# Adaptive modulation moved from TensorE, in the mixers, to GpSimd, in the feed-forwards

## The chip, the cores and the metric

One core of one Trainium2 chip. The metric is the device time of the whole program in microseconds; lower is better. The engines are TensorE (PE; its weight load is listed apart as PEld), VectorE (DVE), ScalarE (ACT), GpSimd (POOL) and SyncE (SP), each with its own instruction stream; they are ordered against each other by semaphores alone, all written out by hand.

## The reference

Two blocks of depth 2 run one after the other on 256 rows of 1024 numbers, all in float32. The first has, per layer, a feed-forward, a hybrid mixer (forgetting attention, stick-breaking attention, a sparse attention with an index step) and a second feed-forward. The second block has neighbourhood attention with a pooling branch in layer 0 and a short convolution in layer 1, each between two feed-forwards, and these are modulated by two condition vectors:

```python
def adaln(cond, w, b):
    m = jax.nn.silu(cond) @ w + b          # cond (D,), w (D, 9*D)
    return m.reshape(m.shape[:-1] + (N_MOD, D_MODEL))

def ffn_sublayer(h, m, g, w13, w2, base):
    hn = modulate(rms_norm(h, g), m[:, :, base], m[:, :, base + 1])
    return h + 0.5 * m[:, :, base + 2] * swiglu_2(hn, w13, w2)

for i in range(DEPTH):
    m_l = adaln(c[:, None, :], mod_w[i], mod_b[i])      # mod_w (2, 1024, 9216)
    m_c = adaln(c_ctx[None, None, :], mod_w[i], mod_b[i])
```

So the modulation is a product of two vectors (`c` and `c_ctx`) with a 1024 x 9216 matrix per layer: 75.5 MB of weights for few arithmetic operations. Of `c_ctx` only the first five of nine parts of layer 0 are needed. Nothing of the modulation depends on the first block, so it may be computed at any time before the second.

## The kernel before

Everything stays in SBUF but the weights. These stream through a ring of three buffers, `raw`, of 1 MB each (a "unit"), loaded from SyncE's queue. Each unit is split into a high and a low part: ScalarE copies it to `whi` (line 415) and VectorE subtracts (`wlo = raw - whi`, line 428, two inputs in SBUF). TensorE then makes each product as three (`three`, line 710: hi by hi, hi by lo, lo by hi). Plain f32 products show in the trace as two passes.

A feed-forward (nine in all) is a loop over 11 groups of 256 hidden columns. One step is three units: two for gate and up, one for down, 72 products of 512 columns. Units of a step are split while earlier ones are used.

The phases of the program stand in a list; every engine walks it. A `norm`, `ffn` or `final` may begin before the phase ahead is over; others wait for all. In a mixer, TensorE's steps of attention are short and wait for other engines, so pieces of other work are put between them by hand: `Beside` holds a list of pieces and `PACE` says how many go at each point. There are three kinds, in the order of the string `BESIDE`:
- `D`, a part of the remaining input projection: 6 products of 512 columns, 4 such per unit, 80 per layer;
- `m`, a modulation vector of 256 columns for both conditions: 8 products with the `silu` of the conditions (`CT`, 32 columns, in four column groups of TensorE at once) as the stationary side and the weights (`mraw`, which lies in the idle tile `C`) as the moving one, then a copy by VectorE (line 1438). The weights come as two loads of 0.5 MB from SyncE's queue (line 605);
- `t`, the turn of that vector so that it lies along the partitions: two products on TensorE (line 772), a sum and the bias on VectorE (lines 1444 and 1445) into `modc`. The next `m` in a mixer waits until that has been read (`settle(unread, "row_read")`).

26 `m` and 26 `t` lie in each of the two hybrid mixers, 20 and 20 in the neighbourhood attention, where no projection is left over. In a hybrid mixer 5 pairs fall before the softmax heads, 12 beside these and 9 beside the stick-breaking heads; the 80 `D` fall 34, 24 and 22. `gains` in a feed-forward (line 1527) multiplies the norm's gains in. GpSimd has the lower 896 columns of a mixer's splits (line 671) and a few small loads.

## Time and profile before

| | |
|---|---|
| median of 3 runs | 2875.26 us (2868.48 to 2882.46) |
| the profiled execution | 2875.02 us |
| its span, first to last instruction | 2873.2 us, mean granted clock 0.958 |
| TensorE busy | 2660.1 us (93%) |
| VectorE, ScalarE, GpSimd busy | 1416.9, 1175.5, 111.3 us |
| products of the modulation, busy | 96.4 us, and 31.6 us of turns |

The nine feed-forwards take about 170 to 190 us each, some 1560 us. The hybrid mixers' attention parts run from 236 to 494 and from 960 to 1217, the neighbourhood attention from about 1984 to 2122. A time is read against the span; the time of an execution is 1.8 us more. "Busy" counts overlapping instructions of an engine once; the mean of one instruction can be longer than its share, since TensorE's are pipelined.

### The profile page before, as it was taken

The numbers are of one execution on the slowest core, as the hardware profiler recorded it, in microseconds if no ns is written. First come the engines' busy times: TensorE is split into PE (matmuls) and PEld (weight loads), VectorE is DVE, ScalarE is ACT, GpSimd is POOL, SyncE is SP. The second block draws the span as 40 slices with busy tenths as digits, with TensorE's granted clock in tenths as the row PEclk, the third lists the DMA queues.
The fourth block names the chain that finished last, engine by engine and source line by source line (L and its number), as shares of the span: only waits on it lengthen the run. The fifth ranks groups of instructions, "written<-read, shape, count | busy, mean of one in ns | idle before, by whom it ended". The sixth has DMA issues, their size and how long they took to land.

```text
span 2873.2 us, 34247 instructions
## 1 busy us (share of the span) xinstructions
PE 2660.1 (93%) x12829; PEld 2107.3 (73%) x12829; DVE 1416.9 (49%) x1830; ACT 1175.5 (41%) x1356; POOL 111.3 (4%) x85
## 2 busy tenths in 40 slices
PE   7999987899999898889989989988889999998998
PEld 6877655688788665568878878875467878876786
DVE  4555334655545643365454454443335555455554
ACT  4445334444443533444444344443024444444433
POOL 0002110000000211000000001000000000000000
PEclk9999999999999999899999999997889999998999
DMA  6556554465555555546545559842555545554453
GB/s 202 189 172 201 174 191 163 147 201 189 165 185 177 185 191 192 167 153 214 187 134 183 185 135 193 213 145 95 169 165 163 188 156 191 185 166 135 162 187 113
DMA packets 367783, 496.16 MB, mean 173 GB/s; under 512 B 14478, under 2 KB 295338, under 8 KB 367562
## 3 DMA queue, kind: packets, MB, share of 16 engines
q1 hardware_dynamic: 365338, 487.99, 51.8%
q0 software_dynamic: 2064, 5.84, 2.3%
q8 instruction: 64, 1.05, 0.2%
q10 hardware_dynamic: 288, 1.05, 0.1%
q14 instruction: 29, 0.24, 0.0%
HBM read 493.77 MB, written 1.05 MB: 172 GB/s over the span
## 4 chain that ended last, share of the span: by engine, by line
PE 85%; DVE 7%; ACT 4%; DMA 3%; issue 1%; ACTq 0%; DVEq 0%; SPq 0%; PEldq 0%
PE ps L710 79%; PE ps L790 2%; DVE wlo L428 2%; PE ps L909 2%; DMA C<-in_mod_w_dram 1%; ACT whi L415 1%; PE ps L797 1%; PE ps L772 1%; DMA raw<-in_w_in_dram 1%; ACT L1319 0%; DVE arena L1473 0%; DMA raw<-in_even_w_out_dram 0%; ACT work L1160 0%; DVE HTlo L1363 0%; DVEq L348 0%
## 5 line engine op out<-in xcount | busy, mean ns | idle before, releaser
L428 DVE TENSOR_TENSOR wlo<-raw,whi 128x2048 fp32r<-128x2048 f32 (+5 forms) x405 | 872.0, 2155 | 611.6 <-ACT whi L415 609.4
L710 PE MATMUL ps<-whi,HThi 128*128 128x512 f32 (+2 forms) x2360 | 956.2, 405 | 33.6 <-DVE HTlo L1479 16.8
L415 ACT ACTIVATE whi<-raw 128x2048 fp32r<-128x2048 f32 (+4 forms) x405 | 752.7, 1860 | 467.9 <-PE ps L710 437.8
L710 PE MATMUL ps<-wlo,HThi 128*128 128x512 f32 (+2 forms) x2360 | 929.6, 394 | 0.0
L710 PE MATMUL ps<-whi,HTlo 128*128 128x512 f32 (+2 forms) x2360 | 929.5, 394 | 0.0
L710 PEld LDWEIGHTS ps<-whi,HThi 128*128 128x128 f32 x2360 | 452.0, 192 | 155.9 <-issue 45.8
L710 PEld LDWEIGHTS ps<-wlo,HThi 128*128 128x128 f32 x2360 | 450.9, 191 | 96.4
L710 PEld LDWEIGHTS ps<-whi,HTlo 128*128 128x128 f32 x2360 | 452.6, 192 | 84.6
L710 PE MATMUL ps<-whi,AThi 128*128 128x512 f32 x792 | 310.1, 391 | 1.1
L710 PE MATMUL ps<-wlo,AThi 128*128 128x512 f32 x792 | 308.6, 390 | 0.0
L710 PE MATMUL ps<-whi,ATlo 128*128 128x512 f32 x792 | 308.1, 389 | 0.0
L710 PEld LDWEIGHTS ps<-whi,AThi 128*128 128x128 f32 x792 | 148.7, 188 | 34.8 <-issue 4.7
L1229 ACT ACTIVATE AThi<-ps 128x512 fp32r<-128x512 f32 x99 | 59.1, 597 | 278.4 <-PE ps L909 278.4
L710 PEld LDWEIGHTS ps<-wlo,AThi 128*128 128x128 f32 x792 | 148.7, 188 | 31.1
L710 PEld LDWEIGHTS ps<-whi,ATlo 128*128 128x128 f32 x792 | 148.8, 188 | 30.2
L1541 DVE TENSOR_TENSOR ATlo<-ps,AThi 128x512 fp32r<-128x512 f32 x99 | 68.3, 690 | 143.7 <-ACT AThi L1229 143.7
L710 PE MATMUL ps<-C,CT 128*32 128x256 f32 x1152 | 96.4, 454 | 42.4 <-DVE modc L1445 26.6
L1136 ACT ACTIVATE work<-ps,small 128x128 f32<-128x128 f32 (+2 forms) x60 | 29.5, 492 | 217.2 <-DVE small L1395 217.0
L1225 ACT ACTIVATE arena<-ps 128x256 f32<-128x256 f32 x110 | 36.2, 381 | 185.9 <-PE ps L710 185.9
L671 POOL TENSOR_TENSOR wlo<-raw,whi 128x896 fp32r<-128x896 f32 x36 | 84.0, 2333 | 391.7 <-ACT whi L415 391.7
L1225 ACT ACTIVATE arena<-ps,small 128x256 f32<-128x256 f32 x88 | 36.9, 470 | 140.8 <-PE ps L710 140.7
L1394 DVE TENSOR_REDUCE small<-ps 128x1 f32<-128x128 f32 (+2 forms) x60 | 26.8, 446 | 132.0 <-PE ps L790 87.8
(191 smaller groups left out, 1589.0 us busy)
## 6 DMA issues: line engine op xcount, KB each, us to landing
raw<-in_ffn_w_dram SPq DMA_DIRECT2D x330, 512.0 KB, 4.5
raw<-in_w_ffn_gu_dram SPq DMA_DIRECT2D x176, 512.0 KB, 4.7
C<-in_mod_w_dram SPq DMA_DIRECT2D x144, 512.0 KB, 4.5
raw<-in_w_ffn_down_dram SPq DMA_DIRECT2D x88, 512.0 KB, 4.0
raw<-in_w_in_dram SPq DMA_DIRECT2D x40, 1024.0 KB, 7.3
raw<-in_even_w_in_dram SPq DMA_DIRECT2D x12, 1024.0 KB, 5.1
raw<-in_conv_w_in_dram SPq DMA_DIRECT2D x12, 1024.0 KB, 5.1
raw<-in_w_out_dram SPq DMA_DIRECT2D x8, 1024.0 KB, 5.0
```

Source lines behind the costliest of these rows:

```text
L415: i = nc.scalar.activation(whi[0:rows, r, a:b], raw[0:rows, r, a:b], ACT.Copy)
L428: i = nc.vector.tensor_tensor(wlo[0:rows, r, a:b], raw[0:rows, r, a:b], whi[0:rows, r, a:b].bitcast(F32), ALU.subtract)
L671: nc.gpsimd.tensor_tensor(wlo[at], raw[at], whi[at].bitcast(F32), ALU.subtract).then_inc(s_lo_pool, 1)
L710: return nc.tensor.matmul(o, lhsT, rhs, start=first, stop=last)
L772: i = nc.tensor.transpose(ps[:, turned, k * P:(k + 1) * P], mrow[:, k * P:(k + 1) * P], ident)
L790: i = nc.tensor.matmul(S[:, o:o + ow], lh, rh, start=False, stop=j == len(mine) - 1)
L797: i = nc.tensor.transpose(T[:, c * P:(c + 1) * P], prob[(n - 1) % 2][:, c * P:(c + 1) * P], ident)
L909: i = nc.tensor.transpose(ps[:, 2, c * SEQ + b * P:c * SEQ + (b + 1) * P], av[:, b, c * P:(c + 1) * P], ident)
L1136: A(prob[n % 2][:, 0:it["n"]], ps[:, n % 2, 0:it["n"]], ACT.Exp, bias=nmx[:, n:n + 1], scale=SCALE, accum_out=rsum[:, n:n + 1]).then_inc(s ...
L1225: A(sg[:, b, :], ps[:, b, 0:GW], ACT.Silu, scale=scale).then_inc(sem("ffn_silu"), 1)
L1229: A(AT[own][0][:], ps[:, 2, :].rearrange("p (c t) -> p c t", c=2), ACT.Copy).then_inc(sem("ffn_act_hi"), 1)
L1541: V.tensor_tensor(AT[own][1][:], ps[:, 2, :].rearrange("p (c t) -> p c t", c=2), AT[own][0][:].bitcast(F32), ALU.subtract).then_inc(sem("f ...
```

## The change

All 72 vectors leave TensorE's streams in the mixers, and `BESIDE`, `m` and `t` are gone; `PACE` now counts `D` alone. GpSimd makes the vectors during the first eight feed-forwards: 10, 6, 8, 12 (layer 0), then 10, 10, 8, 8 (layer 1). It loads half of a vector's weights (4 x 128 rows by 256 columns) from its own queue, multiplies each of the four blocks by the condition's column (`tensor_scalar`), adds the blocks, and adds both halves into `acc`: 128 x 256 partial sums, one row per partition. For the first 20 vectors of layer 0 it does so for both conditions, so there are 92 such sums. Vector i of a feed-forward begins no earlier than a step given by the count of used units. TensorE waits at the end of each such feed-forward until its vectors are made. The sum over the partitions is then made by TensorE: 128 columns of `acc` as the stationary side, a column of ones as the moving one, 184 products of one column in six places. VectorE adds the bias and multiplies the gains in (`mod_add`). The bias tiles of the neighbourhood attention are now loaded between the vectors of the sixth feed-forward.

```diff
-BESIDE = ("mDDDDDDDDt" * 4 + "mDtDmDtDmDtDmDtD" * 5 + "mDtDmDDDtDDD",) * 2 + ("m" + "tm" * 19 + "t",)
-PACE = (dict(prepare=8, latent=(4, 2), turn_index=3, index=(4, 4, 4, 4, 4, 3), softmax=4, item=(2,), stick=6),) * 2 + (dict(item=(2, 2, 3)),)
+PACE = dict(prepare=7, latent=(3, 2), turn_index=2, index=(3, 3, 3, 3, 3, 3), softmax=3, item=(1,), stick=3)
...
+        mods = [modulation(l, first, last, slots[f]) for f, (l, first, last) in enumerate(
+            ((0, 0, 10), (0, 10, 16), (0, 16, 24), (0, 24, 36), (1, 0, 10), (1, 10, 20), (1, 20, 28), (1, 28, 36)))]
+        made_by = [sum(len(acc) for part in mods[:f + 1] for _, _, acc in part) for f in range(len(mods))]
+        shares = {f: (made_by[f], [x for g in fs for x in mods[g]])
+                  for f, fs in ((0, (0,)), (2, (1, 2)), (3, (3,)), (4, (4,)), (5, (5,)), (7, (6, 7)))}
...
-                        elif what == "mod":
-                            load_mod(m)
-                            load_mod(m + 1)
...
+            def modulate(ph, at, beside):
+
+                part = ph["mods"]
+                for i in range(2):
+                    mod_load(part, i, at)
+                for i in range(2 * len(part)):
+                    _, m, accs = part[i // 2]
+                    if i % 2 == 0:
+                        pool.wait_ge(s_used, ph["u0"] + 3 * (10 * (i // 2) // len(part)) + 2)
+                        beside(i // 2)
+                    halves[0] += 1
+                    pool.wait_ge(s_mod[i % 2], 16 * ((halves[0] + 1) // 2))
+                    for st, acc in reversed(list(enumerate(accs))):
+                        w = mod_raw[at][i % 2]
+                        o = w if st == 0 else mod_product
+                        for c in range(4):
+                            k = 4 * (i % 2) + c
+                            p = nc.gpsimd.tensor_scalar(o[:, MOD * c:MOD * (c + 1)], w[:, MOD * c:MOD * (c + 1)],
+                                                        cond[:, k, st:st + 1], None, ALU.mult)
+                        link(p)
+                        link(nc.gpsimd.tensor_tensor(o[:, 0:2 * MOD], o[:, 0:2 * MOD], o[:, 2 * MOD:4 * MOD], ALU.add))
+                        if i % 2 == 0:
+                            link(nc.gpsimd.tensor_tensor(acc, o[:, 0:MOD], o[:, MOD:2 * MOD], ALU.add))
+                        else:
+                            link(nc.gpsimd.tensor_tensor(acc, acc, o[:, 0:MOD], ALU.add))
+                            link(nc.gpsimd.tensor_tensor(acc, acc, o[:, MOD:2 * MOD], ALU.add))
+                    if i % 2:
+                        pool.sem_inc(s_made, len(accs))
+                    if i + 2 < 2 * len(part):
+                        mod_load(part, i + 2, at)
...
+            def mod_sums(share, bank):
+
+                settle(summed, "mods_added")
+                made, parts = share
+                pe.wait_ge(s_made, made)
+                at = 0
+                for _, m, accs in parts:
+                    for k in range(MOD // P):
+                        for acc in accs:
+                            i = mm(ps[:, bank, at:at + 1], acc[:, k * P:(k + 1) * P], cc("ones"))
+                            at += 1
+                i.then_inc(sem("mods_summed"), 1)
...
                 if ph["gate"]:
                     take("gate_read")
+                if ph["mods"]:
+                    pe.wait_ge(s_made, made_by[f])
+                if ph["sums"]:
+                    mod_sums(ph["sums"], 3)
...
                     turn(rest_chunks(), "rest_turned", ("rest_read", "rest_read"))
+                    mod_sums(ph["sums"], 5)
                     take("forget_log")
...
                     beside.go(next(quota))
+                    mod_add(ph["sums"], 5)
                     take("forget_summed")
```

GpSimd's stream at the first feed-forward, where it had nothing; after the change (`arena` holds the weights, the products and the partial sums):

```order
L660 DMA arena<-in_mod_w_dram 128x4x256
L679 TENSOR_SCALAR arena<-arena,cond 128x256 x4
L682 TENSOR_TENSOR arena<-arena 128x512
L684 TENSOR_TENSOR arena<-arena 128x256
L679 TENSOR_SCALAR arena<-arena,cond 128x256 x4
L682 TENSOR_TENSOR arena<-arena 128x512
L684 TENSOR_TENSOR arena<-arena 128x256
```

That is the first half of one vector for both conditions; the second half has one more addition of 256 for each. The first feed-forward has ten such vectors.

TensorE in the neighbourhood attention, before: the four score products of an item, `m` (`C,CT`), `t` (L772), the turns of the item ahead (L797) and its value products (128x64):

```order
L710 MATMUL ps<-arena 128x256
L790 MATMUL ps<-arena,cst 128x256
L790 MATMUL ps<-cst 128x256
L710 MATMUL ps<-arena 128x256
L797 MATMUL ps<-cst,work 128x128 x4
L710 MATMUL ps<-arena,work 128x64 x4
L710 MATMUL ps<-C,CT 32x256 x8
L772 MATMUL ps<-cst,work 128x128 x2
L710 MATMUL ps<-C,CT 32x256 x8
```

And after:

```order
L742 MATMUL ps<-arena 128x256
L816 MATMUL ps<-arena,cst 128x256
L816 MATMUL ps<-cst 128x256
L742 MATMUL ps<-arena 128x256
L823 MATMUL ps<-cst,work 128x128 x4
L742 MATMUL ps<-arena,work 128x64 x4
L742 MATMUL ps<-arena 128x256
```

Nothing stands between the items any more.

TensorE at the end of a hybrid mixer's index step, layer 0, before: the turns of the heads (L727), the forget gate's sums (128x6), its turn (L1037), then `m`:

```order
L772 MATMUL ps<-cst,work 128x128 x2
L727 MATMUL ps<-cst,arena 128x128 x16
L727 MATMUL ps<-cst,arena 64x128 x2
L727 MATMUL ps<-cst,arena 128x128 x4
L727 MATMUL ps<-cst,arena 64x128 x2
L710 MATMUL ps<-small,cst 128x6 x3
L1037 MATMUL ps<-cst,small 6x128 x2
L710 MATMUL ps<-C,CT 32x256 x8
```

And after:

```order
L759 MATMUL ps<-cst,arena 128x128 x16
L759 MATMUL ps<-cst,arena 64x128 x2
L759 MATMUL ps<-cst,arena 128x128 x4
L759 MATMUL ps<-cst,arena 64x128 x2
L742 MATMUL ps<-cst,arena 128x1 x40
L742 MATMUL ps<-small,cst 128x6 x3
L1070 MATMUL ps<-cst,small 6x128 x2
```

40 one-column products now stand ahead of the gate's sums; 48 do in layer 1.

## Rows read from the trace of the kernel before

**Rows 1.** Stretches: length, busy us (x instructions) per engine, granted clock, DMA share, GB/s.

```profile
core 0: us, PE busy (x) PEld busy (x) DVE busy (x) ACT busy (x) POOL busy (x), PEclk, DMA share, GB/s
24.00:213.00 189.00, 185.38 (x832) 152.30 (x832) 95.12 (x74) 80.07 (x72) 0.00 (x0) 0.99 0.55 182
...
312.00:412.00 100.00, 96.51 (x607) 63.92 (x611) 39.98 (x124) 30.07 (x61) 12.57 (x6) 0.98 0.64 211
412.00:494.00 82.00, 62.27 (x368) 42.92 (x365) 29.75 (x75) 34.88 (x47) 6.33 (x3) 0.86 0.49 159
...
1460.00:1498.00 38.00, 27.26 (x115) 22.19 (x114) 19.39 (x28) 20.35 (x32) 0.00 (x0) 0.82 0.22 73
...
2005.00:2126.00 121.00, 101.23 (x626) 60.35 (x626) 38.19 (x105) 12.21 (x32) 0.00 (x0) 0.77 0.54 174
```

**Rows 2.** Chain of waits, second feed-forward: start, us, what.

```profile
604.44 16.35 PE ps L710 x72
621.22 16.35 PE ps L710 x72
```

**Rows 3.** Timeline of one feed-forward step: start, us, engine, line, instruction.

```profile
606.91 2.29 DVE L428 TENSOR_TENSOR wlo<-raw,whi 128x2048 fp32r<-128x2048 f32 x1 [1.11 <-ACT whi L415]
...
614.96 0.19 PEld L710 LDWEIGHTS ps<-whi,AThi 128*128 128x128 f32 x1
```

**Rows 4.** Instruction groups: busy us, mean ns, idle before and releaser.

```profile
L710 PE MATMUL ps<-C,CT 128*32 128x256 f32 x1152 | 96.4, 454 | 42.4 <-DVE modc L1445 26.6 <-DMA C<-in_mod_w_dram 11.2 <-DVEq L348 2.1
...
L702 POOL DMA_DIRECT2D work<-in_pool_w_dram x1 | 0.8, 754 | 0.0
...
L1818 POOL MEMSET const-float32-1.0<- 128x1 f32 x1 | 0.1, 98 | 0.0
```

**Rows 5.** Timeline, softmax heads.

```profile
320.61 1.07 PE L710 MATMUL ps<-C,CT 128*32 128x256 f32 x16
...
321.61 0.50 PE L710 MATMUL ps<-whi,HThi 128*128 128x512 f32 x1
...
325.42 0.39 PE L772 MATMUL ps<-cst,work 128*128 128x128 f32 x2
```

**Rows 6.** Waits of TensorE from 412 to 494: us, times, longest.

```profile
PE ps L710 <- DVE modc L1445: 9.6, 2, 5.7
```

**Rows 7.** Timeline, stick-breaking heads, of ScalarE and of TensorE.

```profile
432.07 0.49 ACT L1317 ACTIVATE work<-ps 128x384 f32<-128x384 f32 x1
...
437.79 0.52 ACT L1326 ACTIVATE work<-work 128x384 f32<-128x384 f32 x1 [1.46 <-DVE work L1738]
...
445.80 0.49 ACT L1317 ACTIVATE work<-ps 128x384 f32<-128x384 f32 x1 [5.68 <-PE ps L710]
...
430.80 0.92 PE L710 MATMUL ps<-arena 64*128 64x256 f32 x4
...
433.36 1.07 PE L710 MATMUL ps<-C,CT 128*32 128x256 f32 x16
```

**Rows 8.** Timeline, neighbourhood attention, items at either speed.

```profile
2001.02 1.22 PE L710 MATMUL ps<-arena 64*128 64x256 f32 x2
...
2007.97 1.94 PE L710 MATMUL ps<-C,CT 128*32 128x256 f32 x16
...
2042.74 0.70 PE L710 MATMUL ps<-arena 64*128 64x256 f32 x2
...
2046.48 1.07 PE L710 MATMUL ps<-C,CT 128*32 128x256 f32 x16
```

**Rows 9.** Timeline, TensorE at the end of layer 0's index step.

```profile
304.14 0.80 PE L710 MATMUL ps<-small,cst 128*128 128x6 f32 x6 [1.45 <-ACT arena L1117]
```

**Rows 10.** Timeline, splits of VectorE and GpSimd side by side.

```profile
249.36 4.53 DVE L428 TENSOR_TENSOR wlo<-raw,whi 128x1152 fp32r<-128x1152 f32 x2
...
292.71 2.02 DVE L428 TENSOR_TENSOR wlo<-raw,whi 128x1152 fp32r<-128x1152 f32 x1
...
249.55 3.13 POOL L671 TENSOR_TENSOR wlo<-raw,whi 128x896 fp32r<-128x896 f32 x1 [3.47 <-ACT whi L415]
...
291.38 2.13 POOL L671 TENSOR_TENSOR wlo<-raw,whi 128x896 fp32r<-128x896 f32 x1 [25.11 <-ACT whi L415]
```

More of the change, by code:

```diff
@@ L252, in program @@
                       for n0 in range(0, 3 * D, 512)]
-            phase("beside", first=len(units), pieces=pieces(BESIDE[l], w, later), pace=PACE[l], end=len(units), banks=(5, 5),
-                  after=0 if l == 0 else c_read)
+            phase("beside", first=len(units), pieces=pieces(w, later), end=len(units))
             for kind in ("prepare", "latent", "turn_index", "index", "softmax", "stick"):
-                phase(kind, l=l)
+                phase(kind, l=l, sums=shares[2 * l] if kind == "index" else None)
             phase("beside_end")
@@ L303, in program @@
                 phase("near_turn")
-                phase("beside", first=len(units), pieces=pieces(BESIDE[2]), pace=PACE[2], end=len(units), banks=(6, 7), after=c_read)
                 phase("near")
-                phase("beside_end")
                 phase("turn", src=[[work[:, 2048 + b * 512 + k * P:2048 + b * 512 + (k + 1) * P] for b in range(NB)]
@@ L1026, in _ @@
                         i.then_inc(sem("index_dots"), 1)
-                    beside.go(sum(beside.pace["index"]))
+                    beside.go(sum(PACE["index"]))
                     settle(taken, "group_taken")
```

255 lines of the change are left out of this document (126 added, 129 removed).

## The prediction

> **What bounds the kernel now.** I read the stretches first. In a feed-forward TensorE is the bound: the chain of waits goes through 72 matmuls per step, one step in 16.78 us (604.44 to 621.22), with VectorE and ScalarE beside it [rows 2]. No modulation work stands there. It stands elsewhere: in a mixer's first part (236 to 312), its softmax heads (312 to 412) and its stick-breaking heads (412 to 494), all three again in layer 1, and the neighbourhood attention (2005 to 2126). TensorE is busy for 96.5 of 100 us in the softmax heads, 62 of 82 in the stick-breaking heads, 101 of 121 in the neighbourhood attention, at a granted clock of 0.77 [rows 1]. So the time of the modulation can be bought only there. The price is paid in the feed-forwards, where GpSimd now does nothing (24 to 213, POOL 0.00 [rows 1]), and where TensorE now waits at the end until GpSimd is through.
>
> **What is removed.** 72 vectors of 256 columns, each 16 products (8 f32 matmuls of two passes; 1152 in all, 16 a vector), one copy and, later, two turns and two small VectorE operations [rows 4]. In TensorE's stream a piece m takes 1.00 us (320.61 to 321.61) and its turn t about 0.25 us of its 0.39, the rest being overlap [rows 5]: 1.25 us for a pair. A mixer holds 26 of them: 5 in the first part, 12 in the softmax heads, 9 in the stick-breaking heads.
> - Softmax heads: TensorE-bound, so 12 x 1.25 = 15 us per layer. What is late next is an item's exponential. It comes from VectorE's maximum of the item before, 0.29 to 0.42 us, and ScalarE's 0.47 us, while TensorE has a projection piece of 1.4 us and its own 2 us to do: covered.
> - First part: 5 x 1.25 = 6 us, and about 3 us in which TensorE waits for the turned row to be read: 9 us per layer.
> - Stick-breaking heads: one head now takes 13.7 us (ScalarE's first step at 432.07, then at 445.80) [rows 7]. In these heads TensorE waits for a modulation row to be read by VectorE, which is behind its head's own chain: 9.6 us in two waits [rows 6]. Without m and t nothing of TensorE's projection pieces waits for VectorE's place in the head. What remains is ScalarE's own round: 6.2 us from its first step to the exponential's end (437.79 and 0.52), plus most of a 1.9 us split and a share of an eviction, about 8.5 us. TensorE has 2.6 us of its own (430.80 to 433.36) and 3 pieces of 1.4, 6.8 us, at full clock and about 11.4 at half. I take 10 us, between the two: 7 rounds x 3.7 = 25 us per layer; bounds 9 x 1.25 = 11 (the waits merely change their name) and 7 x 5.2 = 36.
> - Both layers: 2 x (15 + 9 + 25) = 98 us.
> - Neighbourhood attention: at full clock an item's own matmuls run from 2042.74 to 2046.48, 3.74 us, without a gap, then its m begins [rows 8]. At half clock its own part is 6.95 us (2001.02 to 2007.97). The same matmul of 256 columns takes 0.70 us in the one and 1.22 in the other: the lower of the two clock levels (1.2 GHz), which this stretch had for nearly half of its time (mean 0.77 [rows 1]), among others after waits for modulation weights, and these go. The 16 items now take the 121 us of that stretch and some 17 ahead of it, with 20 m among them. After: 5 or 6 items at 7 us, the other 10 or 11 at 3.75, and 5 us of tail, about 85 us: 50 us gained. Bounds: all at half speed 117 + 5 (gain 16), nearly all at full speed (gain 70).
> Removed: 148 us.
>
> **What TensorE gets instead.** 184 products of one column, two passes each. The nearest row is six passes of 128x6 in 0.80 us, 0.13 each, 0.27 us a product [rows 9]. 40 of them stand at the end of layer 0's index step, 48 of layer 1's, right before the sums of the forget gate that the softmax heads wait for: 10.7 and 12.8 us on the path, and 1.2 us each for VectorE's additions, which stand ahead of the gate's copy: 26 us. 32 stand ahead of the convolution: 8 us. 24 in the final norm are hidden, since TensorE is idle in 11 of 38 us there (1460 to 1498 [rows 1]); 1 us. 2 x 20 at feed-forward ends lie half in the norm's chain: 6 us. Added: 41 us. Bounds: 15 us (all hidden but the index steps' own) to 60 (half clock).
>
> **What GpSimd must do, and when.** A vector for one condition is 8 tensor_scalar of 256, 2 additions of 512, 3 of 256, and 7 waits for its own result. The one elementwise row is the 896-wide subtraction: 2.13 us undisturbed (291.38 [rows 10]). With 0.10 us fixed (the memset [rows 4]) that is 2.27 ns per column: 1.26 us for 512, 0.68 for 256. No row has a tensor_scalar here. It costs at least the memset's 0.10 and at most the 0.68 of two inputs; I take 0.38, half the slope for one input instead of two. A wait I put at 0.10 (between nothing and 0.25; no row shows one). So 8 x 0.38 + 2 x 1.26 + 3 x 0.68 + 0.7 = 8.3 us; two conditions and two DMA issues of 0.75 (as the 128x4-run load of rows 4) make 18 us, one condition 9.7.
> The GPSIMD Engine Reference of the Trainium skill (Engine selection) says that one-input work is roughly line-rate; by that a tensor_scalar would be near 0.32 us (an estimate from that page), and the stall below some 10 us shorter.
>
> These don't run undisturbed. At 249.55 a subtraction of GpSimd took 3.13 us instead of 2.13, begun just behind a VectorE split (249.36). At 291.38 it was GpSimd that had begun, and the split begun at 292.71, until 294.73, ended 1.2 us after GpSimd's end at 293.51 [rows 10]. Whoever begins second stands still until the first is through. A feed-forward step has three splits of 2.29 us [rows 3], 2.2 of them holding: 6.6 of 16.8 us are lost to GpSimd. VectorE loses at most one GpSimd operation per split, 1.3 us, and has over 5: the split begun at 606.91 ended at 609.20, and its unit is first used at 614.96 [rows 3]. So TensorE does not feel it within a step.
> The Trainium skill's page SBUF — State Buffer (Who interferes with whom) says the same, that a VectorE operation with two SBUF inputs and a reading GpSimd operation exclude each other; the two rows above agree. It speaks against this change: by the reverse, no lock, the stall below would be about 10 us instead of 82.
>
> The sum, feed-forward by feed-forward. In the first, 10 vectors for both conditions need 180 us. From 36 (two units used) to 212 (its end) are 176 us, less 10.5 steps x 6.6 = 107 free. 73 us are missing; TensorE stands still, the splits stop, and GpSimd runs undisturbed, 3 us of it beside the norm: 70 us. Later ones have 171 - 67 = 104 us free. Needs: 108 (6 double), 111 (4 double, 4 single), 116 (12 single), 97, 117 (10 single and 32 small DMAs of about 0.6 us), 78, 78. Waits for loads and results partly fall under the splits, so the deficits of 4 to 13 us come to about 12 us in all. Stall: 82 us. The long stop at 212 also lets the clock fall; in 1460 to 1498, with 11 idle us, the mean was 0.82, so some 13 of 38 us were at the lower level [rows 1]: 7 us.
>
> **Sum.** 2875.0 (this execution, span 2873.2; the median of three is 2875.3) - 148 + 41 + 82 + 7 = 2857 us. Nothing is gained on the feed-forwards' weights; 144 loads of 0.5 MB move from the mixers' queue to GpSimd's, and a feed-forward then moves 182 GB/s and some 60 more; the softmax heads do 211 [rows 1]. I put no cost, and up to 10 us in the range.
>
> **Rivals.**
> 1. GpSimd keeps up (tensor_scalar near 0.1 to 0.2 us, or it slips between the splits). Stall 0 to 40 us, no slow clock behind it: 2875 - 148 + 41 + 20 = 2788 us. For it: the bounds allow it. Against: rows 10, and 180 us of need in 176.
> 2. The other side: GpSimd is the bound of the first six feed-forwards. With 0.5 us and more for a tensor_scalar and 0.15 to 0.25 for a wait, a double vector takes 21 to 24 us; the first stall is 95 to 125 us and the next ones 15 to 40 each, 140 to 290 together: 2875 - 107 + 7 + 180 = 2955 us. It turns slower than before from a stall of 100 us on, a tensor_scalar of 0.45 us. For it: short operations of unknown fixed cost and 7 self-waits. Against: only the memset's 0.10 us.
> 3. TensorE idles in the mixers and the clock stays low: stick-breaking saves 11, not 25, per layer, the neighbourhood attention 16, not 50, the products cost 60: 2857 + 28 + 34 + 19 = 2938 us. For it: 0.86 and 0.77 granted there already [rows 1]. Against: the waits that go are those after which it fell.
>
> **Chances.** The forecast 0.45 (2825 to 2890: of it 0.27 faster by over 0.5%, 0.12 within, 0.06 slower), rival 1 0.22 (faster), rival 2 0.20 (slower), rival 3 0.13 (0.03 within, 0.10 slower). 0.5%, 14 us, is about what a measurement of this kernel can tell from none. Together faster 0.49, same 0.15, slower 0.36. The range must reach from rival 1 into rival 2: 2775 to 2955. The forecast's own range is 2825 to 2890.
>
> **What would show it.** A GpSimd tensor_scalar of 0.3 to 0.45 us when alone; a stop of TensorE of 50 to 90 us behind the first feed-forward, with GpSimd busy through it, and stops under 15 us behind the next; feed-forward steps still of 16.8 us; softmax pairs of items 1.2 us shorter; stick-breaking rounds near 10 us; neighbourhood attention about 50 us shorter; 40 one-column products in 10 to 11 us. The forecast is wrong if there is no such stop, if a step grows (VectorE then pays for the lock), or if the mixers don't shrink.

## The result

The changed kernel takes **3175.19 us** (median of four, 3168.26 to 3180.6) against 2872.48 (median of four): a ratio of 1.105, 95% interval 1.101 to 1.109. The forecast was 2857 us and the range went to 2955: the time lies outside it, 318 us above the forecast. The profiled execution has a span of 3178.7 us at a mean granted clock of 0.891; before it was 2873.2 us at 0.958.

The page of the changed kernel (engines; slices of the span; the chain of work that ended last; groups of GpSimd's products):

```profile
PE 2657.7 (84%) x11901; PEld 2163.6 (68%) x11901; DVE 1431.8 (45%) x1617; ACT 1172.4 (37%) x1354; POOL 1778.6 (56%) x1425
...
POOL 5999611039979961104995995995000997960000
PEclk9985689899979978989996996996957999998999
...
PE 46%; POOL 42%; DVE 4%; issue 3%; ACT 3%; DMA 1%; ACTq 0%; DVEq 0%; SPq 0%; POOLq 0%; PEldq 0%
...
L679 POOL TENSOR_SCALAR arena<-arena,cond 128x256 f32<-128x256 f32 x736 | 902.1, 1238 | 91.8 <-PE ps L742 77.6
...
L682 POOL TENSOR_TENSOR arena<-arena 128x512 f32<-128x512 f32 x184 | 318.1, 1729 | 15.4
```

GpSimd is now 42% of the chain that set the end, and more than half of that is one line, the multiplication of 256 columns by a condition: 736 of them, 1.24 us each. What waits is TensorE. Its waits, summed (us, times, longest), and the first one's end in the timeline:

```profile
PE ps L908 <- POOLq L689: 240.4, 3, 155.7
PE ps L742 <- POOLq L689: 121.9, 3, 54.3
```
```profile
364.99 1.97 PE L908 MATMUL ps<-cst,X 128*128 128x128 f32 x8 [155.67 <-POOLq L689]
```

POOLq L689 is GpSimd's count of finished vectors: TensorE stood still 362 us in six waits, 156 of them behind the first feed-forward. Two stretches, the first feed-forward's steps (the one that answers [rows 1], 24 to 213) and the stop behind it:

```profile
core 0: us, PE busy (x) PEld busy (x) DVE busy (x) ACT busy (x) POOL busy (x), PEclk, DMA share, GB/s
24.00:200.00 176.00, 174.53 (x791) 144.28 (x792) 91.27 (x66) 75.52 (x70) 158.59 (x116) 1.00 0.66 217
212.00:360.00 148.00, 0.00 (x0) 0.00 (x0) 1.69 (x1) 0.00 (x0) 137.67 (x150) 0.51 0.13 43
```

In the steps TensorE is as busy as before; then it does nothing for 148 us while GpSimd works alone. The six waits, in order: 155.7, 40.6, 44.1, 54.3, 31.2 and 36.4 us.

The rest of the change did much of what it should. Lengths of stages, worked out from the starts of the same instructions in each timeline (us; e1_little and e2_bcast are experiments below):

| stage | before | changed | e1_little | e2_bcast |
|---|---|---|---|---|
| ten steps of feed-forward 1 | 165.2 | 166.8 | 166.8 | 165.2 |
| feed-forward 0's last step to layer 0's latent | 54.7 | 208.8 | 54.4 | 143.4 |
| behind 1 / behind 2 | 27.0 / 53.1 | 68.3 / 96.2 | 27.0 / 52.4 | 29.7 / 53.0 |
| behind 3 / behind 4 | 39.3 / 37.6 | 97.3 / 71.7 | 39.3 / 37.5 | 53.8 / 36.7 |
| behind 5, to attention's first exponential | 122.6 | 160.7 | 121.1 | 118.1 |
| latent to forget gate, layer 0 / 1 | 48.5 / 46.9 | 63.0 / 66.7 | 60.7 / 64.0 | 63.1 / 64.4 |
| softmax heads, layer 0 / 1 | 80.2 / 80.3 | 65.9 / 65.9 | 65.9 / 65.9 | 65.9 / 65.9 |
| stick-breaking starts, layer 0 / 1 | 57.9 / 57.8 | 34.9 / 34.7 | 33.9 / 34.2 | 34.8 / 33.8 |
| neighbourhood attention, first to last exponential | 116.6 | 98.2 | 98.2 | 98.2 |
| behind 7, to the convolution | 89.6 | 99.9 | 99.8 | 99.7 |

### The profile page after: what moved, and what is told of

The parts are those of the page before. It is cut to its first block, busy times and chain, and to the rows that moved or that the text cites. A ratio compares the mean times of both kernels' runs of the same rounds, so it can differ in the third digit from the quotient of the medians.

```text
span 3178.7 us, 33443 instructions
## 1 busy us (share of the span) xinstructions
PE 2657.7 (84%) x11901; PEld 2163.6 (68%) x11901; DVE 1431.8 (45%) x1617; ACT 1172.4 (37%) x1354; POOL 1778.6 (56%) x1425
## 4 chain that ended last, share of the span: by engine, by line
PE 46%; POOL 42%; DVE 4%; issue 3%; ACT 3%; DMA 1%; ACTq 0%; DVEq 0%; SPq 0%; POOLq 0%; PEldq 0%
PE ps L742 42%; POOL arena L679 23%; POOL arena L682 8%; POOL arena L686 3%; POOL arena L684 3%; POOL arena L660 3%; PE ps L816 2%; POOL arena L687 2%; PE ps L823 1%; POOL arena L703 1%; ACT whi L417 1%; DVE wlo L430 0%; PE ps L937 0%; PE ps L908 0%; DVE arena L1524 0%
## 5 line engine op out<-in xcount | busy, mean ns | idle before, releaser
L430 DVE TENSOR_TENSOR wlo<-raw,whi 128x2048 fp32r<-128x2048 f32 (+5 forms) x405 | 923.4, 2282 | 600.7 <-ACT whi L417 598.8
L679 POOL TENSOR_SCALAR arena<-arena,cond 128x256 f32<-128x256 f32 x736 | 902.1, 1238 | 91.8 <-PE ps L742 77.6
L660 POOL DMA_DIRECT2D arena<-in_mod_w_dram x144 | 116.1, 806 | 464.5 <-DVEq L350 393.4
L682 POOL TENSOR_TENSOR arena<-arena 128x512 f32<-128x512 f32 x184 | 318.1, 1729 | 15.4
L908 PE MATMUL ps<-cst,X 128*128 128x128 f32 x96 | 16.6, 333 | 242.1 <-POOLq L689 240.4
L908 PEld LDWEIGHTS ps<-cst,X 128*128 128x128 f32 x96 | 13.8, 173 | 245.7 <-issue 241.7
L742 PE MATMUL ps<-cst,arena 128*128 128x1 f32 x368 | 73.2, 335 | 126.3 <-POOLq L689 121.9
L742 PEld LDWEIGHTS ps<-whi,AThi 128*128 128x128 f32 x792 | 148.7, 188 | 34.9 <-issue 4.7
```

What stands on the lines that cost most here:

```text
L430: i = nc.vector.tensor_tensor(wlo[0:rows, r, a:b], raw[0:rows, r, a:b], whi[0:rows, r, a:b].bitcast(F32), ALU.subtract)
L660: pool.dma_start(dst, kn(t["mod_w_2"][l], 4 * (i % 2), 4, m * MOD, MOD)).then_inc(s_mod[i % 2], 16)
L679: p = nc.gpsimd.tensor_scalar(o[:, MOD * c:MOD * (c + 1)], w[:, MOD * c:MOD * (c + 1)], cond[:, k, st:st + 1], None, ALU.mult)
L682: link(nc.gpsimd.tensor_tensor(o[:, 0:2 * MOD], o[:, 0:2 * MOD], o[:, 2 * MOD:4 * MOD], ALU.add))
L742: return nc.tensor.matmul(o, lhsT, rhs, start=first, stop=last)
```

## The experiments

The theory at the outset (P): the price of GpSimd's arithmetic, with the lock of VectorE's splits on top, makes TensorE wait, and that alone turned the change round. Its rivals were losses in the mixers, the number of instructions and self-waits (waits of GpSimd for its own last result), and the transfers. Two side questions were the neighbourhood attention's clock and the price of the one-column products.

### e1_little: nearly no arithmetic

```diff
-                        for c in range(4):
...
-                        link(nc.gpsimd.tensor_tensor(o[:, 0:2 * MOD], o[:, 0:2 * MOD], o[:, 2 * MOD:4 * MOD], ALU.add))
...
+                            link(nc.gpsimd.tensor_tensor(acc, w[:, 0:MOD], w[:, MOD:2 * MOD], ALU.add))
...
+                            link(nc.gpsimd.tensor_tensor(acc, acc, w[:, 0:MOD], ALU.add))
```

> GpSimd still loads every piece, but of the products and sums of a half only one 256-column addition is left (the modulation's values are left out). Theory P (GpSimd's arithmetic is too dear and all that the change lost is TensorE waiting for it): a state vector falls from 12.5 us undisturbed to about 1.5 us, TensorE's 362 us of waits for GpSimd go, and the time is about 3175 - 362 = 2813 us, 2795 to 2830. Rival M (the mixers, the clock and the one-column products lost as much): 2850 us or more.

Measured: **2811.8 us**, 0.975 of before (0.968 to 0.983); no wait for GpSimd is left. It is 363 us under the changed kernel, and TensorE's waits there were 362. The table says the same stage by stage: everything behind the feed-forwards is back at its old length. So the loss is GpSimd's arithmetic. The other parts of the change, its loads too, are worth 2.5% together. Rival M falls, though three stages lie above what I had forecast without a stop: the two index steps and the attention.

### e2_bcast: one multiplication of 1024 columns for four of 256

```diff
-                        for c in range(4):
...
+                        link(nc.gpsimd.tensor_tensor(
+                            o.rearrange("p (c n) -> p c n", c=4), w.rearrange("p (c n) -> p c n", c=4),
+                            cond[:, 4 * (i % 2):4 * (i % 2) + 4, st].unsqueeze(2).broadcast_to([P, 4, MOD]), ALU.mult))
```

> The four 256-column multiplications of a half (3.62 us undisturbed) become one 1024-column multiplication by the four conditions repeated along the columns. Theory P, with two-input operations at 1.26 us for 512 columns: 2.5 us, so a state vector takes 10.3 us in place of 12.5, GpSimd's busy time falls by about 295 us, of which TensorE waits for four fifths: about 2935 us, 2890 to 2990. Rival N (the number of instructions and self-waits is what costs): from 16 to 10 instructions of a state vector, the state vector falls by over a third and the time to 2860 us or less. Rival D (the landing of the weights is what GpSimd waits for): within 20 us of 3175.

Measured: **2917.0 us**, 1.012 of before (1.004 to 1.020), 258 us below the changed kernel, within the range of theory P. Rival D falls; N's price (a vector over a third cheaper, 2860 us or less) isn't reached. GpSimd undisturbed (TensorE stopped), the changed kernel and e2_bcast (start, us, instruction):

```profile
290.85 3.62 POOL L679 TENSOR_SCALAR arena<-arena,cond 128x256 f32<-128x256 f32 x4
294.56 1.26 POOL L682 TENSOR_TENSOR arena<-arena 128x512 f32<-128x512 f32 x1
295.89 0.72 POOL L684 TENSOR_TENSOR arena<-arena 128x256 f32<-128x256 f32 x1
296.91 0.81 POOL L660 DMA_DIRECT2D arena<-in_mod_w_dram  x1 [0.30 <-POOL arena L684]
```
```profile
286.17 1.90 POOL L677 TENSOR_TENSOR arena<-arena,cond 128x1024 f32<-128x1024 f32 x1
288.14 1.26 POOL L680 TENSOR_TENSOR arena<-arena 128x512 f32<-128x512 f32 x1
289.48 0.72 POOL L682 TENSOR_TENSOR arena<-arena 128x256 f32<-128x256 f32 x1
```

Four multiplications with one input take 3.62 us, 0.905 each; one with two inputs over the same 1024 columns takes 1.90. A vector for one condition now needs 2 x 1.90 + 2 x 1.26 + 3 x 0.72 + 7 x 0.08 = 9.0 us in place of 12.5, and the forecast had 8.3. This makes e2_bcast nearly the kernel that the prediction had worked out, and its waits of TensorE for GpSimd stand beside the 82 us forecast:

```profile
PE ps L906 <- POOLq L687: 92.0, 2, 89.8
...
PE ps L740 <- POOLq L687: 11.1, 1, 11.1
```

89.8 us behind the first feed-forward (forecast 70) and 13 behind the others (forecast 12).

### e3_immediate and e4_one_wide: what makes the multiplication dear

```diff
-                                                        cond[:, k, st:st + 1], None, ALU.mult)
+                                                        0.5, None, ALU.mult)
```

> The multiplications of GpSimd take the constant 0.5 in place of the condition's column (the conditions are left out of the modulation). Theory C (reading the per-partition column costs the excess over the 0.38 us that was forecast): a multiplication takes 0.35 to 0.5 us undisturbed, and the time falls to about 2850 to 2900 us. Rival R (the operation has this rate whatever its scalar is): four still take 3.6 us undisturbed and the time stays within 20 us of 3175.

```diff
-                        for c in range(4):
...
+                        link(nc.gpsimd.tensor_scalar(o, w, cond[:, 4 * (i % 2), st:st + 1], None, ALU.mult))
```

> One multiplication of 1024 columns by one condition stands for the four of 256 (three of four conditions are left out). Theory R (a rate per column, 3.5 ns): 3.3 to 3.6 us undisturbed, and the time is 3140 to 3175 us. Rival F (a fixed cost for each instruction of 0.5 us or more, then the 1 ns per column): 1.5 to 2.1 us, and the time falls below 2950 us.

Measured: 3140 us and 2967 us, one execution each. The timelines of e3_immediate and e4_one_wide, undisturbed:

```profile
288.01 3.30 POOL L679 TENSOR_SCALAR arena<-arena 128x256 f32<-128x256 f32 x4
```
```profile
287.62 2.86 POOL L677 TENSOR_SCALAR arena<-arena,cond 128x1024 f32<-128x1024 f32 x1
```

With a constant a multiplication takes 0.82 us, with the column 0.905: the column is not the cause, and e3's 35 us lie between its two theories, far nearer to R. One of 1024 columns takes 2.86 us against 3.62 for four of 256, so a fixed part is (3.62 - 2.86) / 3 = 0.25 us and the rest 2.5 ns a column. Neither R nor F of e4_one_wide holds as it stood: the rate per column is most of it, and yet the time fell 208 us, since 0.76 us on each of 184 half vectors, and what the lock adds, went from an engine that is behind. The two-input operations give (1.26 - 0.72) / 256 = 2.1 ns a column and 0.18 us fixed. So the operation with one tensor input is the dearer one here.

### e5_no_split: the lock alone

```diff
-                        split_lo(dve, u0 + 3, lead)
+                        split_bit(u0 + 3)
...
-                        split_lo(dve, u0 + 4, lead)
-                        split_lo(dve, u0 + 5, lead)
+                        split_bit(u0 + 4)
+                        split_bit(u0 + 5)
```

split_bit subtracts 64 columns with the same waits and counts.

> The changed kernel, with VectorE's splits in the feed-forward steps cut from 2048 to 64 columns (the low parts of most of the feed-forwards' weights are left out). Theory L (a long two-input operation of VectorE holds GpSimd off the memory): GpSimd's multiplications fall from 1.24 us in the mean to 0.91 and its 512-column additions from 1.73 to 1.26, a state vector takes 12.5 us everywhere, only the first feed-forward's 20 vectors (250 us) are still late, and the time is 2850 to 2880 us. Rival T (the transfers into the buffers, or something else that runs all the time, slow GpSimd down): the means stay within 10% of 1.24 and 1.73, and the time above 3100 us.

Measured: 2910.9 us in one execution. Of the waits for GpSimd 103.4 us behind the first feed-forward and one of 1.9 later are left (the stage behind the first has 155.7 us in place of 54.7, 101 more). The groups of GpSimd in it:

```profile
L679 POOL TENSOR_SCALAR arena<-arena,cond 128x256 f32<-128x256 f32 x736 | 673.4, 929 | 177.2 <-PE ps L742 161.2
L682 POOL TENSOR_TENSOR arena<-arena 128x512 f32<-128x512 f32 x184 | 236.9, 1288 | 15.4
```

929 ns for 1238 and 1288 for 1729: with the splits gone GpSimd's operations are back at their undisturbed price everywhere, while the transfers into the same memory go on. Theory L holds and T falls; only the 2850 to 2880 us was too low, because I had left out, in the 250 us, the loads' issues and the idle time ahead of them: from GpSimd's first product at 35.0 to its last at 312.4 lie 277 us, of them 15 of issues and 8 idle before these. The lock in the changed kernel, a GpSimd addition of 1.26 us that began 0.23 us behind a split:

```profile
70.56 2.29 DVE L430 TENSOR_TENSOR wlo<-raw,whi 128x2048 fp32r<-128x2048 f32 x1 [1.11 <-ACT whi L417]
70.79 3.21 POOL L682 TENSOR_TENSOR arena<-arena 128x512 f32<-128x512 f32 x1
```

So each of the two factors, taken away alone, removes some 258 of the 362 us of waits (103.1 are left in e2_bcast, 105.3 in e5_no_split). They don't add up: what counts is how far a feed-forward's vectors go beyond its length.

### e6_even: the load spread

```diff
-            ((0, 0, 10), (0, 10, 16), (0, 16, 24), (0, 24, 36), (1, 0, 10), (1, 10, 20), (1, 20, 28), (1, 28, 36)))]
+            ((0, 0, 7), (0, 7, 14), (0, 14, 22), (0, 22, 36), (1, 0, 10), (1, 10, 20), (1, 20, 28), (1, 28, 36)))]
```

Four of its vectors lie where layer 1's projections are written before they are summed, so their values are not the modulation's; the work is whole.

> e2_bcast with the first four feed-forwards' state vectors shared 14, 14, 14, 14 in place of 20, 12, 12, 12. In e2_bcast the first one's 20 vectors took 297 us, 14.8 each, and ended 89 us late. Theory P (only the load of a feed-forward against its length matters): 14 vectors take 207 us, of which 170 to 195 lie beside the feed-forward and what surrounds it; each of the four is 10 to 35 us late, 80 in sum in place of 106, and the time is 2885 us, 2860 to 2910. Rival E (what lies between the feed-forwards gives GpSimd the room that it needs): under 10 us late each, and 2840 us or less.

Measured: 2920.1 us, 1.014 of before (1.011 to 1.017), 10 us above what theory P allowed. The stages behind feed-forwards 0 to 3 are 27, 23, 25 and 39 us longer than before, 113 in sum, where e2_bcast has 89, 3, 0 and 15. The expectation's 297 us (14.8 a vector) for e2_bcast's first 20 vectors is too much: from GpSimd's first product at 35.7 to its last at 300.0 they took 264, 13.2 each. Spreading the load gains nothing as long as each feed-forward gets more than about 12 vectors.

### e7_filler, e11_fill2, e14_fill4: the clock in the neighbourhood attention

In the changed kernel TensorE never idles in this stage once the items have begun, and yet its clock stays at the lower of the two levels (1.2 GHz). It falls in the step ahead of them, where TensorE waits, and does not come up again. Windows of the changed kernel, of e7_filler and of e14_fill4:

```profile
2290.00:2294.00 4.00, 3.05 (x20) 2.56 (x19) 1.94 (x6) 1.65 (x6) 0.00 (x0) 1.00 0.13 44
...
2298.00:2302.00 4.00, 1.70 (x4) 0.80 (x4) 1.71 (x5) 0.83 (x2) 0.00 (x0) 0.73 0.00 0
2302.00:2306.00 4.00, 4.00 (x9) 2.34 (x8) 0.55 (x1) 0.00 (x0) 0.00 (x0) 0.50 0.00 0
...
2310.00:2322.00 12.00, 12.00 (x32) 7.33 (x31) 2.78 (x7) 1.55 (x4) 0.00 (x0) 0.50 0.00 0
...
2346.00:2358.00 12.00, 12.00 (x36) 8.08 (x35) 2.93 (x6) 1.46 (x4) 0.00 (x0) 0.50 0.00 0
```
```profile
2088.00:2100.00 12.00, 12.00 (x64) 7.03 (x62) 2.60 (x6) 1.56 (x4) 0.00 (x0) 1.00 0.00 0
```
```profile
2050.00:2054.00 4.00, 4.00 (x11) 1.78 (x11) 1.54 (x3) 0.78 (x2) 0.00 (x0) 0.50 0.00 0
2054.00:2058.00 4.00, 4.00 (x13) 1.77 (x11) 0.00 (x0) 0.00 (x0) 0.00 (x0) 0.76 0.00 0
2058.00:2062.00 4.00, 4.00 (x23) 2.55 (x24) 1.44 (x3) 0.78 (x2) 0.00 (x0) 1.00 0.00 0
...
2120.00:2132.00 12.00, 12.00 (x65) 7.67 (x65) 3.62 (x7) 1.55 (x4) 0.00 (x0) 1.00 0.00 0
```

The fillers (eight in e7_filler, two in e11_fill2, four in e14_fill4, an item):

```diff
+                    if not places:
+                        for _ in range(8):
+                            mm(ps[0:32, 6, 0:MOD], ident[:, 0:32], X[:, 0, 0:MOD])
                     beside.item(n)
```

> e2_bcast with eight products of 256 columns and 32-column weights behind each item's own in the neighbourhood attention, of the shape of the modulation's products in the kernel before (a filler, its result is not read). Theory W (TensorE's granted clock rises there with these products among the items, as it did before): full clock from some 30 us in, and from the first exponential to the last about 117 us as before, 19 more than without the filler. Rival S (the clock stays at half for another reason): items of 6.95 + 3.8 = 10.8 us, 150 us from first to last.

> e2_bcast with two filler products of 256 columns behind each item's own in the neighbourhood attention, where e7_filler had eight and the clock was full throughout, with 108.6 us from the first exponential to the last for 98.2 without filler. Theory W (wide products keep the clock up, the items themselves take some 4.3 us at full clock): 0.85 us of filler for each of the 14 item periods, 70 to 80 us in place of 98.2, and the time is about 2895 us. Rival V (it takes more of them): the clock stays at half and the items grow to 7.9 us, 110 us, the time about 2930.

> e2_bcast with four filler products an item. Theory W (wide products keep the clock up): at 1.00 the two of e12_all took 71.3 us from first to last exponential and the eight of e7_filler 108.6, so four take about 84 us, in every execution: the time is 2903 us, with no executions 60 us above the others, as e11_fill2 had them. Rival V (the clock's coming up there is by chance of the state it enters in): executions of two kinds again, the slow ones with a near stage of 140 us or more, 2960.

Measured, first to last exponential: none 98.2 us, eight 108.6, four 85.7. With eight and with four the clock fell in the step ahead as well, but came up to 1.00 again among the first items (from 2064 and 2058 on) and stayed there. Eight more products an item cost 10 us and four gain 12.5. With two it is either: e11_fill2's profile has 126.2 us at 0.50 throughout, e12_all's below has 71.3, at 1.00 from 1980 on, with the same fillers.

One item follows the other every 4.73, 5.59 and 7.31 us with two, four and eight fillers at 1.00, so 0.43 for a filler, and every 6.95 and 8.79 us with none and two at 0.50. By that an item without fillers would take 3.87 us at full clock (an estimate; no run without fillers reached it), and 14 items at full in place of half clock would be worth some 43 us. The 32 us that the forecast's term lacked are the 10 or 11 items that it had at full clock. Windows of e11_fill2 and of e12_all:

```profile
2102.00:2114.00 12.00, 12.00 (x37) 7.79 (x37) 3.07 (x6) 1.56 (x4) 0.00 (x0) 0.50 0.00 0
```
```profile
2014.00:2026.00 12.00, 12.00 (x63) 7.50 (x63) 4.64 (x11) 2.33 (x6) 0.00 (x0) 1.00 0.01 1
```

The executions of e11_fill2 are of two kinds accordingly, seven from 2876 to 2898 us (median 2888.8, 1.003 of before, 1.001 to 1.005) and four from 2947 to 2960 (the profile is of the second kind; the 55 us between the two stages are most of the difference). e12_all, with two fillers as well, had one of six executions at 2919.5 us, the others from 2841 to 2857; that it is of this kind isn't shown, since it has no profile. The executions of e14_fill4 are all within 2901 to 2913, at a median of 2904.7, 1.010 of before (1.007 to 1.013), and with e13_best's five there are nine executions with four fillers and none of the slower kind; e7_filler took 2947 us in one execution, of which only 10 us more than e2_bcast lie in this stage, 5 behind it, and the others in small differences of stages that the edit does not touch.

### e8_sums_ffn and e9_spread: the one-column products

In the index steps of the changed kernel (timeline of TensorE, and windows of the run and behind it):

```profile
454.26 15.06 PE L742 MATMUL ps<-cst,arena 128*128 128x1 f32 x80 [1.45 <-ACT arena L1154]
```
```profile
454.00:456.00 2.00, 1.74 (x16) 1.77 (x16) 0.00 (x0) 1.83 (x2) 0.00 (x0) 1.00 0.26 96
...
458.00:460.00 2.00, 2.00 (x11) 2.00 (x11) 0.00 (x0) 0.00 (x0) 0.24 (x1) 0.50 0.01 4
460.00:470.00 10.00, 10.00 (x48) 10.00 (x49) 0.45 (x3) 0.00 (x0) 0.00 (x0) 0.50 0.00 0
470.00:482.00 12.00, 11.45 (x38) 7.97 (x38) 2.29 (x5) 1.45 (x2) 0.00 (x0) 0.70 0.00 0
```

40 products, 80 passes, 15.06 us, where 10.7 were forecast from the row of six passes [rows 9]. The clock was at 1.00 from 454 to 456, when the run began, and at 0.50 from 458 on, with TensorE busy without a gap between; 16 passes are seen in the first of these windows and 11 in the second.

```diff
-                  mods=mods[f] if f < len(mods) else [], sums=shares[f] if f in (4, 5) else None)
+                  mods=mods[f] if f < len(mods) else [], sums=shares[f] if f in (0, 2, 4, 5) else None)
...
-                    mod_sums(ph["sums"], 5)
```

> e2_bcast with the one-column products of the two index steps (15.1 us of TensorE at half clock each) moved to the ends of the feed-forwards ahead of them. Theory K (the clock there made them dear): the index steps get 14 us shorter each, the ends of the feed-forwards grow by 40 x 4 x 0.05 = 7 us each or less, and the time falls by 15 to 25 us against e2_bcast's 2917, to about 2897. Rival Z (they cost TensorE the same wherever they stand): 2917 within 5 us.

Measured: 2921.6 us, 1.016 of before (1.012 to 1.019). The index steps got 17 us shorter each, the ends of the feed-forwards 16 and 23 longer. There, too, the run was at half clock, though the clock was 1.00 when it began, behind wide products and 2.7 us of waiting for GpSimd (timeline of e8_sums_ffn up to and from 1000, layer 1's 48 products, whose 96 passes run from 999.28 to 1018.65, and windows):

```profile
999.28 4.01 PE L740 MATMUL ps<-cst,arena 128*128 128x1 f32 x24 [2.68 <-POOLq L687]
...
999.84 18.82 PE L740 MATMUL ps<-cst,arena 128*128 128x1 f32 x91
```
```profile
998.00:1000.00 2.00, 0.72 (x7) 0.75 (x7) 1.86 (x2) 0.00 (x0) 1.01 (x2) 1.00 0.00 0
...
1005.00:1015.00 10.00, 10.00 (x48) 10.00 (x48) 0.00 (x0) 0.00 (x0) 0.00 (x0) 0.50 0.04 15
```

```diff
+                for at, col in enumerate(cols):
+                    if pieces and at % -(-len(cols) // pieces) == 0:
+                        beside.go(1)
+                    i = mm(ps[:, bank, at:at + 1], col, cc("ones"))
```

> e2_bcast with the 40 and 48 one-column products of the index steps laid among the step's projection pieces, three behind each, in place of one run behind them. In e8_sums_ffn their run took 17 to 19 us at the end of a feed-forward too, at a granted clock of 0.50, though the clock ahead of it was 1.00. Theory K (a long run of one-column products is what the clock falls in): among wide products they take half, some 8 us, and the wide products behind them are not slowed: the index steps get 9 to 12 us shorter each, and the time is about 2897 us. Rival Z (they cost TensorE the same wherever they stand): 2917 within 5 us.

Measured: **2893.0 us**, 1.007 of before (1.005 to 1.010), 24 us under e2_bcast, of which some 20 lie in the index steps that the edit touches: 53.1 and 54.8 us for 63.1 and 64.4. A run of three products (six passes) took 0.72 us, 0.12 a pass (timeline). Windows of e9_spread through the index step:

```profile
367.74 0.72 PE L740 MATMUL ps<-cst,arena 128*128 128x1 f32 x6
```
```profile
362.00:374.00 12.00, 12.00 (x71) 10.46 (x70) 10.62 (x39) 1.51 (x1) 0.00 (x0) 1.00 0.57 191
374.00:386.00 12.00, 11.21 (x74) 10.87 (x73) 3.68 (x4) 4.95 (x4) 3.27 (x1) 1.00 0.33 113
```

The same products at a granted clock of 1.00 throughout: K holds and Z falls, and moving the run somewhere else, which had been my reading of it in e8_sums_ffn, is no cure.

### e10_sched, e12_all, e13_best: a version that gains

Some of the modulation is read late: layer 0's last third ahead of feed-forward 6, layer 1's thirds ahead of 7, in the convolution and ahead of 8. The schedule of e10_sched (the slots change with it, and the vectors of feed-forward 6 are summed at its own end):

```diff
-            ((0, 0, 10), (0, 10, 16), (0, 16, 24), (0, 24, 36), (1, 0, 10), (1, 10, 20), (1, 20, 28), (1, 28, 36)))]
+            ((0, 0, 6), (0, 6, 11), (0, 11, 16), (0, 16, 24), (0, 24, 36), (1, 0, 12), (1, 12, 24), (1, 24, 36)))]
```

> e2_bcast with the modulation made by its deadlines: 12, 10, 10, 12, 12, 12, 12, 12 state vectors in feed-forwards 0 to 7 in place of 20, 12, 12, 12, 10, 10, 8, 8 (layer 0's last twelve are first read ahead of feed-forward 6, layer 1's by thirds from feed-forward 7 on). Theory P (a feed-forward covers about 12 vectors at 13 to 15 us, and each one more costs its own time): of e2_bcast's 106 us behind feed-forwards 0 to 3 under 10 are left, feed-forward 5, which loads the bias tiles too, is 5 to 20 us late, and the time is about 2825 us, 2805 to 2850. Rival E (the load is only moved: 92 vectors at their mean of about 15 us are late wherever they are, 6 to 15 us behind each of the eight): 2880 us or more.

> e9_spread, e10_sched and e11_fill2 in one kernel. If each does what its theory says and they add up: 2917 - 20 - 92 - 22 = 2783 us, 2765 to 2805. If the schedule is only moved load: 2840 us or more.

Measured: e10_sched 2891.7 us, 1.006 of before (1.003 to 1.008), 67 us above what P gave. Of the 106 us behind feed-forwards 0 to 3, 88 went (18 are left), as P has it. But behind 4, 5, 6 and 7 it lost 19, 21 (and 6 in the steps of 5), 25 and 10 us against e2_bcast, with TensorE waiting for GpSimd 70 us in six waits, 7.9 of them behind feed-forward 0: 12 vectors for one condition are 24 loads of half a megabyte, where 12 for two conditions are 12, and behind 6 stands a new run of 24 one-column products. So E holds for the second half. That the transfers count there is seen in e1_little, which has hardly any arithmetic: feed-forward 5, which also loads the bias tiles, had 176.1 us for its ten steps in place of 167.0, with the DMA engines full:

```profile
1717.00:1734.00 17.00, 14.25 (x61) 11.46 (x60) 6.23 (x6) 4.85 (x5) 5.66 (x9) 0.93 1.03 231
```

e12_all took **2852.1 us**, 0.990 of before (0.988 to 0.993). It beats the kernel before by 1%, and lies 69 us above its forecast by the same second half, in the range that its expectation gave for a load only moved. The schedule of e13_best, against e12_all's:

```diff
-            ((0, 0, 6), (0, 6, 11), (0, 11, 16), (0, 16, 24), (0, 24, 36), (1, 0, 12), (1, 12, 24), (1, 24, 36)))]
+            ((0, 0, 6), (0, 6, 12), (0, 12, 18), (0, 18, 28), (0, 28, 36), (1, 2, 12), (1, 12, 24), (1, 24, 36)))]
+        mods[4] += modulation(1, 0, 2, slots[4][8:])
```

> e12_all with 12, 12, 12, 12, 10, 10, 12, 12 state vectors in place of 12, 10, 10, 12, 12, 12, 12, 12, and four filler products in the neighbourhood attention in place of two. Theory P (12 vectors fit beside feed-forwards 0 to 3, which have 27 to 55 us behind their steps, but not beside 4 and 5): the two vectors fewer save 10 to 18 us behind each of feed-forwards 4 and 5, at most 5 come in behind 1 and 2, and two more fillers cost 12 us: 2840 us, 2825 to 2850. Rival E (the load is only moved): 2864 us, e12_all's 2852 and the filler's 12.

e13_best, with two vectors fewer beside each of feed-forwards 4 and 5 and two more beside each of 1 and 2, took **2841.5 us**, 0.987 of before (0.984 to 0.989), the fastest with the whole computation in it. Behind 4 stand 36.7 us in place of e12_all's 55.1, to the attention 132.7 for 138.5, the steps of 5 are 170.8 for 180.4, and behind 1 and 2 come in 1.4 and 1.2. Layer 1's index step, with 48 products again for 40, takes 57.9 for 53.0, and the attention with its four fillers 85.8 for 71.3. Theory P holds for this step. 46.5 us of waits for GpSimd are left, in five.

## Why the prediction was wrong

**The step that failed is the price of a tensor_scalar**: "It costs at least the memset's 0.10 and at most the 0.68 of two inputs; I take 0.38, half the slope for one input instead of two." It takes 0.905 us for 256 columns undisturbed, above the upper bound. The bound rested on a ratio of inputs for which no row spoke: the only elementwise row had two inputs, and one input was taken to be no dearer. The page GPSIMD Engine Reference of the Trainium skill (Engine selection), which calls one-input work roughly line-rate, pointed the same way; 0.905 us against 0.72 for two inputs contradicts it. The other prices of the vector held: 512 columns 1.26 us (forecast 1.26), 256 columns 0.72 (0.68), a self-wait 0.08 (0.10), a load's issue 0.81 (0.75).

**The lock** was right, the mechanism and the size: whoever begins second stands still, TensorE doesn't feel VectorE's loss (ten steps 166.8 us, as in e1_little without GpSimd's arithmetic). The Trainium skill's SBUF — State Buffer (Who interferes with whom) has this rule, and e5_no_split shows it by taking the splits away. With a price near the forecast's the stall is the forecast's: e2_bcast 103 us against 82. At 12.5 us a vector the same sum gives: for the first feed-forward some 270 us of need (a double vector near 27 with its two loads) against 107 free, 163 short, measured 155.7. It was rival 2 that came, and its own price (0.5 us and more) stopped short too: it had 140 to 290 us of stalls (95 to 125, then 15 to 40 each), and there were 362 (156, then 31 to 54 each).

**The neighbourhood attention**: 50 us forecast, 18 measured, 16 being my lower bound (all at half speed). The size of an item at either clock was right: 6.95 us from one to the next at half, and 3.87 by the estimate above at full, for 3.75 ([rows 8]; TensorE in the changed kernel, the first matmuls of two items):

```profile
2345.04 1.22 PE L742 MATMUL ps<-arena 64*128 64x256 f32 x2
...
2352.00 1.22 PE L742 MATMUL ps<-arena 64*128 64x256 f32 x2
```

What failed is rival 3's dismissal, "the waits that go are those after which it fell": the waits among the items went, but the clock had fallen ahead of the first item (2298 to 2302), and it did not come up without them. The modulation's wide products among the items went with them, and with four or eight products of 256 columns put back behind an item it came up.

**The one-column products**: 15.1 and 18.8 us for 10.7 and 12.8. The row gave the price at full clock rightly (0.13 us a pass, and 0.12 in e9_spread); what failed is the clock: it was at half for nearly all of their run, and for the forget gate's few products behind it too. The index steps and what is ahead of them grew by 14.5 and 19.8 us, where the forecast had some 4 each (13 for the products, less 9 for the first part). Ahead of the convolution 10 us for 8.

**What held**: softmax heads 14.3 us a layer (15). The stick-breaking heads gained 29 us a layer (25): 57.9 to 34.9 from the first to the last of the five heads' starts, 1.7 ahead of the first and 4.7 and 4.1 behind the last. This is in part luck: the forecast had seven equal rounds, each 3.7 us shorter, 10 in place of 13.7. Of the four between the starts those that took 13.8, 15.4, 13.7 and 15.1 us take 5.1, 13.3, 8.5 and 8.0, 5.8 less in the mean, and the three rounds behind them gained under 5 us together. The third of the four, ScalarE's first step in two heads of the changed kernel:

```profile
572.32 0.49 ACT L1354 ACTIVATE work<-ps 128x384 f32<-128x384 f32 x1 [4.59 <-PE ps L742]
...
580.83 0.49 ACT L1354 ACTIVATE work<-ps 128x384 f32<-128x384 f32 x1 [0.46 <-PE ps L742]
```

**The sum of the misses**: the six stages from a feed-forward's last step to what follows it grew by 369 us (table), where the forecast had 82 of stall, 7 of slow clock and 7 of sums: +273; attention +32; index steps and first part 34 - 8 = +26; stick-breaking -8, behind the attention -5, softmax and convolution +3. Together 321; the two profiled executions lie 305.5 us apart where -18 was forecast, 323.5. No run shows the slow clock's 7 us by itself. The sums at the ends of feed-forwards 4 and 5, forecast at 6 us, cost nothing in e1_little (37.5 us for 37.6, 121.1 for 122.6).

## What to carry to other kernels

- Before work goes to an engine that has done none of its kind, the price of one instruction must be bounded by a row of the same instruction. Where there is none, the upper bound is not the next dearest row that one thinks of; a single instruction of that form, timed beside the kernel, would have settled this case.
- An engine's load is to be compared with the free time stage by stage: nothing is lost up to the edge, and every microsecond beyond it stops the engine that waits. Here two quite different remedies removed nearly the same 258 us of waits, and shares by deadline did more than even ones.
- When work is taken out from among others, look at what the clock did with it there. A stage of small products can lose through the lower clock what the removed ones had cost.

## What the runs showed of the hardware that was not expected

- GpSimd, f32, 128 partitions, undisturbed: multiplication by a per-partition column 0.905 us for 256 columns and 2.86 for 1024; by a constant 0.82 for 256; two inputs 0.72 for 256, 1.26 for 512; and 1.90 for 1024 where one input repeats each value 256 times, less than the 2.34 that the two others give when continued. To spell a multiplication by a column as one with two inputs halves it here.
- In a long run of one-column f32 products, TensorE busy without a gap, the granted clock fell from 1.00 to 0.50 soon after the run had begun (changed kernel, between 456 and 458; e8_sums_ffn, between 1000 and 1002) and stayed there, 0.19 to 0.22 us a pass; in threes among wide products they went at 1.00 and 0.12 us a pass.
- The items of the neighbourhood attention, again without a gap, stood at 0.50 for 98 us. Four unread products of 256 columns behind each made the stage 12.5 us shorter, with the clock back at 1.00 from 2058 on in e14_fill4 (it had stood at 0.50 from 2042 to 2054). With two fillers one kernel ran either way, some 60 us apart. Whether it is the width of the products or something else in them that brings the clock up is left open: no run varied the width.
